# Adding the experts' down-projection bias: in the first expert's combine, or between the sixteenth and the seventeenth

## The reference

```python
logits = (h @ w_router + b_router)
top_val, top_idx = lax.top_k(logits, 4)            # of 32 experts
gates = softmax(top_val)
# for every chosen expert e of a token:
gt = min(h @ w_gate[e] + b_gate[e], 7)
up = clip(h @ w_up[e] + b_up[e], -7, 7)
y  = ((up + 1) * gt * sigmoid(1.702 * gt)) @ w_down[e] + b_down[e]
x  = x + sum over the four experts of gates * y
```

## Time and profile before

| | |
|---|---|
| median of 3 runs | 1285.31 us (1284.87 to 1285.60) |
| the profiled execution's own time | 1284.87 us |
| its span, first to last instruction | 1283.1 us |
| PE busy | 1219.5 us (95% of the span) |
| PE weight loads busy | 560.7 us (44%) |
| DVE busy | 475.3 us (37%) |
| ACT busy | 187.3 us (15%) |
| HBM read | 424.8 MB, 334 GB/s over the span |
| mean granted TensorE clock | 0.984 of full speed |

### The profile page before, as it was taken

One profiled execution on the slowest core, in us unless ns is written; L12 is line 12 of the kernel. 1 busy time (PEld: TensorE's weight loads), 2 busy tenths in 40 slices (PEclk: granted clock), 3 DMA queues, 4 the chain that ended last, 5 costly groups with the idle time before them and its releaser, 6 DMA issues.

```text
span 1283.1 us, 20534 instructions
## 1 busy us (share of the span) xinstructions
PE 1219.5 (95%) x8084; PEld 560.7 (44%) x8084; DVE 475.3 (37%) x1037; ACT 187.3 (15%) x369; POOL 61.5 (5%) x103
## 2 busy tenths in 40 slices
PE   7999899998999999999999999999999999999995
PEld 5667689865333333333333333333333333333332
DVE  5748753232362323322333233232323322332334
ACT  2352224122200100100100010000100100100011
POOL 0204350010000000000000000000000000000000
PEclk9999899999999999999999998999999999999998
DMA  9321300284999999999999999999999999999992
GB/s 262 113 69 42 127 16 5 71 288 164 371 415 403 422 422 422 422 421 421 422 421 423 422 422 422 395 419 422 422 422 421 422 422 422 422 422 422 422 421 79
DMA packets 82002, 428.60 MB, mean 334 GB/s; under 512 B 16287, under 2 KB 30031, under 8 KB 32798
## 3 DMA queue, kind: packets, MB, share of 16 engines
q1 hardware_dynamic: 80522, 427.80, 82.4%
q10 hardware_dynamic: 1436, 0.16, 0.1%
HBM read 424.80 MB, written 3.11 MB: 334 GB/s over the span
## 4 chain that ended last, share of the span: by engine, by line
PE 75%; DVE 2%; ACT 2%; issue 1%; DVEq 0%
PE bank L1671 51%; PE bank L1710 7%; PE bank L1651 7%; PE bank L1658 3%; ACT arena L1516 1%; PE bank L1609 1%; PE bank L1556 1%; PE bank L1679 1%; PE bank L1724 1%; DVE arena L1937 0%; PE bank L1614 0%; PE bank L1546 0%; DVE arena L1965 0%; DVE arena L1957 0%; DVE arena L1888 0%
## 5 line engine op out<-in xcount | busy, mean ns | idle before, releaser
L1671 PE MATMUL bank<-ring,arena 128*64 128x512 f32 x2048 | 456.2, 598 | 19.8 <-ACT arena L1516 17.8
L1671 PEld LDWEIGHTS bank<-ring,arena 128*64 128x64 f32 x2048 | 144.2, 137 | 307.5 <-issue 306.9
L1671 PE MATMUL bank<-arena 128*64 128x512 f32 x1024 | 225.4, 592 | 0.0
L1671 PEld LDWEIGHTS bank<-arena 128*64 128x64 f32 x1024 | 73.4, 136 | 140.6 <-issue 138.2
L1937 DVE TENSOR_TENSOR arena<-arena,bank 128x512 f32<-128x512 f32 (+1 forms) x192 | 117.5, 680 | 16.1 <-PE bank L1710 16.1
L511 PE MATMUL bank<-arena,ring 128*128 128x336 f32 x352 | 103.5, 452 | 1.1 <-DVE arena L645 1.1
L1651 PE MATMUL bank<-arena 128*64 128x512 f32 (+1 forms) x396 | 92.2, 600 | 2.3 <-DVE arena L1818 1.1
L1710 PE MATMUL bank<-arena 64*128 64x512 f32 (+1 forms) x384 | 91.1, 604 | 3.2
L1864 DVE TENSOR_SCALAR arena<-arena 96x64 bf16<-96x64 f32 x33 | 8.3, 250 | 217.5 <-PE bank L1671 217.5
L511 PEld LDWEIGHTS bank<-arena,ring 128*128 128x128 f32 x352 | 67.0, 192 | 34.7 <-issue 1.9
L1925 DVE TENSOR_SCALAR arena<-bank 128x512 f32<-128x512 f32 x32 | 22.1, 691 | 155.4 <-PE bank L1679 155.4
(11 more groups left out here) (352 smaller groups left out, 855.5 us busy)
## 6 DMA issues: line engine op xcount, KB each, us to landing
ring<-in_w_gate_dram SPq DMA_DIRECT2D x128, 1024.0 KB, 12.3
arena<-in_w_up_dram SPq DMA_DIRECT2D x128, 1024.0 KB, 15.4
ring<-in_w_down_dram SPq DMA_DIRECT2D x128, 1024.0 KB, 13.9
ring<-in_w_in_dram SPq DMA_DIRECT2D x11, 1024.0 KB, 5.4
ring<-in_w_out_dram SPq DMA_DIRECT2D x4, 1024.0 KB, 8.6
arena<-in_x_prompt_dram SPq DMA_DIRECT2D x2, 512.0 KB, 5.0
out_wkv_sample_dram<-arena SPq DMA_DIRECT2D x4, 256.0 KB
arena<-in_x_prompt_dram SPq DMA_DIRECT2D x2, 448.0 KB, 4.2
```

The lines of the kernel that those rows point to most:

```text
L1671: mm = M.matmul(bank[64 * hb:64 * hb + 64, b, :], tokens(cc), w[:, c, 512 * hb:512 * hb + 512], start=(cc == 0), stop=(w3 == 2 and cc == K ...
```

## The change

`down_bias` goes, and with it its two semaphores, the wait for DVE, DVE's six adds and the split of the loop. In its place the first pass gets the work. TensorE turns the gates after `turn(xg)`, ACT copies them after its copy of the down product, and each of the six combine matmuls of the first pass is followed by a bias matmul into the same bank, which accumulates onto it (`start=False`). DVE's usual six adds of the first pass then carry both.

```diff
-                def body(n):
+                def body(n, first=False):
                     act.wait_ge(F["t1_ready"], n + 1)
...
                     act.wait_ge(unit_used, n * EU + (UPRE + EU))
                     A.copy(ys, bank[:, 2, :]).then_inc(F["ys_ready"], 1)
-
-                body(0)
-                with act.Fori(1, HALF) as it:
-                    body(it)
-                act.wait_ge(F["gt_turned"], 1)
-                A.copy(gT32[0:NE, :], bank[0:NE, 5, 0:NT]).then_inc(F["gt_ready"], 1)
-                with act.Fori(HALF, NE) as it:
+                    if first:
+                        act.wait_ge(F["gt_turned"], 1)
+                        A.copy(gT32[0:NE, :], bank[0:NE, 5, 0:NT]).then_inc(F["gt_ready"], 1)
+
+                body(0, True)
+                with act.Fori(1, NE) as it:
                     body(it)
...
                     turn(xg).then_inc(F["x_done"], 1)
+                    if first:
+                        for i, (t0, m) in enumerate(TILES):
+                            mm = M.transpose(bank[0:NE, 5, t0:t0 + m], gates[0:m, i, :], ident[0:m, 0:m])
+                        mm.then_inc(F["gt_turned"], 1)
                     pe.wait_ge(F["pgt_ready"], n + 1)
                     pe.wait_ge(F["ys_ready"], n + 1)
+                    if first:
+                        pe.wait_ge(F["bdown_in"], 16)
+                        pe.wait_ge(F["gt_ready"], 1)
                     for i, (t0, m) in enumerate(TILES):
                         for hb in range(2):
                             o = bank[0:m, CMB_BANKS[2 * i + hb], :]
-                            M.matmul(o, PgT[64 * hb:64 * hb + 64, i, 0:m], ys[64 * hb:64 * hb + 64, :],
-                                     start=True, stop=True).then_inc(F["cmb_done"], 1)
-
-                def down_bias():
...
+                            mm = M.matmul(o, PgT[64 * hb:64 * hb + 64, i, 0:m], ys[64 * hb:64 * hb + 64, :],
+                                          start=True, stop=not first)
+                            if first:
+                                mm = M.matmul(o, gT32[0:NE, t0:t0 + m], bdown[0:NE, 512 * hb:512 * hb + 512],
+                                              start=False, stop=True)
+                            mm.then_inc(F["cmb_done"], 1)
...
-                with pe.Fori(1, HALF) as it:
-                    body(it)
-                down_bias()
-                with pe.Fori(HALF, NE) as it:
+                with pe.Fori(1, NE) as it:
                     body(it)
...
-                with dve.Fori(1, HALF) as it:
-                    body(it)
-                for i, (t0, m) in enumerate(TILES):
-                    for hb in range(2):
-                        k = 2 * i + hb
-                        dve.wait_ge(F["bd_done"], k + 1)
-                        o = acc[0:m, i, 512 * hb:512 * hb + 512]
-                        V.tensor_tensor(o, o, bank[0:m, CMB_BANKS[k], :], ALU.add).then_inc(F["bd_read"], 1)
-                with dve.Fori(HALF, NE) as it:
+                with dve.Fori(1, NE) as it:
                     body(it)
```

More of the change, by code:

```diff
@@ L1318, in build @@
             "acc_turned", "acc_ready", "ms_ready", "rms_ready", "wrg_ready", "ssum_done", "logits_done",
-            "rstd_ready", "h_ready", "gat_done", "xg_ready", "bdown_in", "gt_turned", "gt_ready", "bd_done", "bd_read",
+            "rstd_ready", "h_ready", "gat_done", "xg_ready", "bdown_in", "gt_turned", "gt_ready",
             "zp_turned", "zp_copied", "top_ready", "ex_ready", "mask_ready", "rank_done", "tab_ready", "bias_split",
@@ L1326, in build @@
         EU = 12
-        HALF = NE // 2
         landed = unit_landed + [lsem(f"ext_landed{i}") for i in range(EXT_SLOTS)]
```

## The result

The changed kernel is slower: median 1300.15 us of 4 runs (1296.65 to 1302.60) against 1285.45 us of 4 runs (1284.87 to 1287.30), ratio 1.011 with a 95% interval of 1.0085 to 1.0136. In a second series on another occasion it was 1301.11 against 1286.50 us, 14.6 us slower, ratio 1.0111 (1.0090 to 1.0132). The forecast was 1291.8 us, 1283.0 to 1294.5: the direction was right, the size was less than half of what came.

A forecast was written before the change was run, and what follows sets the result against it. TensorE's own work was taken to set the pace from expert 2 on. -13.7 + 0.75 + 15.9 + 2.0 - 1.9 + 3.5 = +6.5 us on 1284.9, plus 0.4 for the median, gave 1291.8 us, range 1283.0 to 1294.5.

The forecast's parts named there:

- The stop goes: Between the two expert loops, at expert 16, TensorE's stop for the separate bias step disappears: -13.7 us.
- The turn of the gates: In expert 0, turning the gates behind turn(xg) and ACT's copy delay the combine: +0.75 us, bounds 0.4 and 1.0.
- The combine: In expert 0, alternating combine and bias matmuls do not pair and the clock falls: 18.7 us, +15.9 over 2.77.
- R2: Rival for expert 0's combine: tiles of different height overlap and the clock stays; -5.5 us, 1279.8 us, chance 0.05.
- R1: Rival for expert 0's combine: the clock stays at full speed throughout; -2.1 us, 1283.2 us, chance 0.15.
- The clock's return: In the product behind expert 0's combine, the clock stays low for a while: +2.0 us, bounds 1.4 to 2.7.
- the table: In expert 1, TensorE's waits for Pm and DVE vanish because DVE keeps up with expert 0's longer combine: -1.9 us.
- The lead: TensorE's lead over up-weight transfers runs out, with waits from about expert 26 on: +3.5 us, bounds 2.5 and 4.5.

The follow-up runs named there:

- nobias: Changed kernel with the down-projection bias left out altogether, so it computes something else; 1281.11 us, ratio 0.9957 to the kernel before.
- rows128: Changed kernel with bias matrix zero-padded to 128 rows and turned gates copied in 128 rows, order kept; 1289.29 us, ratio 1.0024 to the kernel before.
- pause: Changed kernel with 13 unused dense matmuls on TensorE between experts 15 and 16; 1307.42 us, ratio 1.0171 to the kernel before.
- grouped: Changed kernel with expert 0's six combine matmuls first and the six bias matmuls behind them; 1286.17 us, ratio 0.9993 to the kernel before.
- paired: Changed kernel with bias matrix and gates padded to 64 rows and held twice, order combine, combine, bias, bias; 1283.70 us, ratio 0.9975 to the kernel before.
- after_mid: Changed kernel with its bias work, same form, moved from expert 0 to expert 16; 1298.81 us, ratio 1.0093 to the kernel before.

## Why the prediction was wrong, step by step

The profile pair puts the failure first in the combine. Its span grew by 11.3 us where the sum had 6.5, with the stop at just the 13.7 us that the sum had for it. What is missing there is 2.5 us from the combine, 1.2 from the lead, 0.6 from the product behind the combine and 0.4 from ahead of expert 0's `gather`, up to rounding. The profiled execution's 1296.7 us are outside the range already. The stop comes on top when medians are compared.

- **The stop goes, -13.7 us.** Wrong in size for the median. One profile had a long stretch of half clock in it; two others have 10.4. The mean of the three is 11.5, and nobias agrees: -11.5, plus 5.4 of late data and 0.4 outside the span (below), is -5.7, measured -5.4 with an interval of -7.3 to -3.9, while with 13.7 it would be -7.9. The step took one execution's figure for the kernel's. What would have warned: half of that stop was a clock that can fall sooner or later.
- **The turn of the gates, +0.75.** Right: `turn(xg)` to the first combine matmul was 1.64 us where it was 0.85, +0.8.
- **The combine, 18.7 us, +15.9.** Right in mechanism, 2.5 us short in size. This is the step that failed. Nothing pairs and the clock falls, 2.7 us in and not 3.5, which is worth 0.6 us. The rest is the price of one matmul: behind a change of tile it takes 1.04 us at full clock and 2.00 at half, not 0.96 and 1.81; a change costs 0.2 and 0.3 us, not 0.1. That 0.1 came from two changes between 64 and 128 rows at the ends of a run of pairs; with a change on both sides of every matmul it did not hold. Measured +18.4, above the upper bound of 17.3. R2 is refuted by the rows of the combine. R1 is refuted here; its clock is what rows128 shows for bias matmuls of full height, at 9.7 us for the combine's growth and not 8.7.
- **The clock's return, +2.0 us, and the table, -1.9.** The table is right, the return is inside its bounds: pass 1 takes 31.78 us, 29.14 and 2.6 for the slow product; the 1.93 us of waits are gone. The rule of the Trainium skill, in "TensorE: Matmul & The Clock Gate", section "Why this matters for your kernels", that gaps between bursts bring the clock down, does not cover this: it fell at 351.2 us with TensorE busy since 348.52, and rows128 had the same 0.6 us of wait before its combine and no fall.
- **The lead, +3.5.** Right in mechanism, measured 4.7 with the first wait at expert 25, over the upper bound of 4.5; in the second profile of the changed kernel it is 3.7. nobias and pause show it from both sides.
- **Sum.** -11.5 + 0.8 + 18.4 + 0.7 (product and table) + 4.7 = +13.1, against +14.6 measured with an interval of 11.6 to 17.0. The forecast's +6.5 lacks 2.2 from the stop, 2.5 from the combine and 1.2 from the lead. Another 0.6 is pass 1, where the product cost 2.6 and not 2.0. Of what lies between 13.1 and 14.6, 0.4 is outside the span: an execution's time is 2.2 to 2.3 us over its span in the changed kernels and 1.8 in the one before. The rest is inside the interval and not traced. The -11.5 rests on three profiles. My range ended at +9.2 because each of these was bounded alone, and the stop that goes was not bounded at all.

## What to carry to other kernels

A matmul that is put between others has to have their tile: with another height it broke the pairing on both sides here, and with 32 rows the clock fell on the way. Putting the bias matmuls behind the combine and not between its matmuls was worth 15 us (grouped against the changed kernel); padding them with zeros to the neighbours' height as well made it 17 (paired). Where work of the bounding engine stands matters when a queue falls slowly behind it: in the profiles the stop in the middle that refills the lead was partly free (late data of 4.7 us gone in after_mid and pause), while nearly all of the 19.9 us at the start was paid (late data of 4.7 us against 5.4 in nobias). The gain from removing a stop that holds a stretch of half clock has a spread, and one profile does not show it.

## What the runs showed of the hardware

With the same order, the same twelve changes of tile and the same 1.04 us for a matmul, bias matmuls of 32 rows had the clock at 0.50 (1.2 GHz) from 351.2 us on, 2.7 us into the combine, and those of 128 rows kept it at 1.00 (2.4 GHz) through all of it. Neither idle time (0.61 and 0.62 us before the combine, none in it) nor busy time tells the two apart. The changes of tile do not either: in grouped there are two of them and the clock fell in a row of 32-row matmuls, while in paired, at the same place, the bias matmuls padded to 64 rows and run in pairs left it at 1.00. Why rows that hold only zeros should count is not shown. A float32 matmul of 64 rows and 512 columns costs 0.43 us when it has a partner in the other 64 rows and 1.04 us when its neighbours have another tile height.
